# Attention in a fused two-block kernel: VectorE adds the first query tile's bias to its scores in PSUM; bias tiles laid out row by row in HBM, the second tile's bias through the identity

## The chip, the cores and the metric

The kernel runs on one core of one Trainium2 chip. The metric is the device time of one execution in microseconds; the numbers given are medians of several executions.

## The reference

Two transformer blocks run one after the other on 256 tokens of width 1024, all in float32. The first is a hybrid (state-space mixer, gated delta rule, mixture of experts). The second has four layers; each is a feed-forward half, a mixer and a second feed-forward half. The mixers alternate: layers 0 and 3 have mixer A, layer 1 a gated MLP, layer 2 mixer C. Only mixers A and C are touched.

```python
# mixer A, 16 heads of 64, chunks of 64 queries
rel  = clip(pad + i - j, -128, 128) + 128          # i: place in the query's chunk, j: place in its band of keys
s    = q @ k.T / 8 + rel_bias[:, rel]
s    = where(valid, s, -1e30); p = softmax(s); o = p @ v
# mixer C, 8 heads, each with two maps of 64
s    = q @ k.T / 8 - slope[h] * abs(qpos - kpos)
s    = where(kpos < (qpos // 64 + 1) * 64, s, -1e30); p = softmax(s)
o    = (p[:, 0] - lam * p[:, 1]) @ v
```

In both, a query sees the keys of its own 64-token chunk and of those before it. The bias depends only on the distance of query and key (and on the head), so the bias of the first 128 queries against the first 128 keys is the same tile as that of the last 128 queries against the last 128 keys.

## The kernel before, in words

Each engine has its own program, and semaphores order them. The large weights come as slabs of 128 x 2048 float32 through SyncE's DMA queue; ScalarE rounds each one to a high part (L385) and VectorE subtracts for the low part (L393), and TensorE multiplies with three products (L406 to L408). This is most of the run.

An attention stage (layers 0, 2 and 3) goes by **turns**: 8 turns of 2 heads (in layer 2: the two maps of one head). A turn g has these steps.

- `scores(g)`, TensorE, lines 2280 to 2300. For each of the 2 heads, in one PSUM bank, four float32 matmuls: the bias of the second query tile (128 queries x 256 keys) through a 128x128 constant (L2296), onto it the scores of that tile (L2297), the bias of the first query tile (128 x 128) through the same constant (L2298), onto it its scores (L2299). The constant, `turn`, is `ident` in layer 2 and `flip` (ones on the other diagonal) in layers 0 and 3. Every float32 matmul shows in the trace as two passes with a weight load each. The two heads of a turn use two banks, and two turns four banks, so `scores(g + 2)` waits for the exponentials of turn g.
- `maxes(g)`, VectorE, lines 2402 to 2408: row maxima of the second tile's scores (L2406) and of the first's (L2407), negated (L2408). The helper `done` makes VectorE wait for its own instruction before it goes on.
- `exps(g)`, ScalarE, L2367: four exponentials with row sums.
- `normalise(g)`, VectorE, lines 2410 to 2420: reciprocals (L2414; L2418 too in layer 2) and two multiplies (L2419, L2420).
- `turned(g)`, TensorE, L2310: six transposes of the probabilities; ScalarE copies them to SBUF (L2390).
- `out_of(g)`, TensorE, L2329 and L2330: the product with the values; ScalarE reads it out (L2374, or L2376 and L2377 in layer 2).

The order of the work is written out by hand for each engine. TensorE does `scores(0)`, `scores(1)`, two slabs of the projection (`mix_cols_pe`), and then for g = 0 to 7: `scores(g + 2)` while there are any, `out_of(g - 1)`, `turned(g)`. ScalarE does, for each g, the high part of a slab of the output weights (g = 0, 2, 4), the copy of the turned tiles of g, `exps(g + 2)`, the read-out of g - 1. VectorE does `normalise(g)`, the low part of that slab (g = 1, 3, 5), `maxes(g + 2)`.

The bias tiles of 2 turns (4 heads, 512 KB) lie in one of two buffers, `bias_a`. GpSimd loads them in `bias_pool` (lines 2246 to 2269) with its own DMA queue. The first two loads have no wait for a buffer; the third and the fourth wait until the turns that used the buffer have their scores (L2255). In layers 0 and 3 the table in HBM, `rel_rows`, has a row of 512 numbers for each head, and each partition reads 256 of them, one place further on than the partition before (L2260 to L2262); this puts the queries upside down, which `flip` puts right. Then GpSimd waits for the load and writes -1e30 over the keys that half of the queries don't see (L2266), and TensorE waits for that (L2285). In layer 2 the table `alibi` has whole tiles with the -1e30 in them (L2257), and TensorE waits for the load alone (L2287).

Of the kernel before, what the change touches and what calls it, by code (L numbers as in the profile page):

```python
# [19 lines left out]
ALU = mybir.AluOpType  # L20
# [3 lines left out]
P = 128  # L24
D = 1024
T = 256
# [10 lines left out]
KINDS = [i % 3 for i in range(LAYERS)]  # L37
# [205 lines left out]
def build(nc, a, out):  # L243
# [3 lines left out]
    def S(name):  # L247
        if name not in sems:
            sems[name] = ctx.enter_context(nc.semaphore(name))
        return sems[name]  # L250
# [4 lines left out]
    with ctx:  # L255
# [22 lines left out]
        rows = scratch[:, 1024:3072].rearrange("p (s n) -> p s n", s=2)  # L278
        sil = scratch[:, 3072:3584]
        h_raw = scratch[:, 3584:4096]  # L280
        mats = sb("mats", [P, len(MATS), P])
        cols = sb("cols", [P, NCOLS])
# [21 lines left out]
        psum = ctx.enter_context(nc.psum_tensor("psum", [P, 8, 512], F32))  # L304
# [3 lines left out]
        def mat(name):  # L308
            return mats[:, MATS[name], :]
# [1850 lines left out]
        SC = T + P  # L2160
# [85 lines left out]
        def bias_pool(pool, l):  # L2246
            n = ATT.index(l)

            pool.wait_ge(S("pre_rstd"), NT * (4 + 3 * l))
            for b in range(4):  # L2250
                bt = 4 * n + b
                s = bt % 2
                if bt >= 2:

                    pool.wait_ge(S("scores"), 2 * (bt - 1))  # L2255
                if KINDS[l] == 2:
                    pool.dma_start(bias_a[s], a["alibi"][:, 4 * b:4 * b + 4, :]).then_inc(S(f"bias_in{s}"), 16)  # L2257
                else:

                    tab = a["rel_rows"]  # L2260
                    base = tab.offset + ((l // 3) * 16 + 4 * b) * 512
                    pool.dma_start(bias_a[s], bass.AP(tensor=tab.tensor, offset=base, ap=[[1, P], [512, 4], [1, T]]))\  # L2262
                        .then_inc(S(f"bias_in{s}"), 16)
                    pool.wait_ge(S(f"bias_in{s}"), 16 * (bt // 2 + 1))

                    pool.memset(bias_a[s][64:P, :, 192:256], -1e30).then_inc(S("bias_ready"), 1)  # L2266
            if KINDS[l] == 0:

                pool.wait_ge(S("bias_ready"), 4 * same_before(l) + 4)
# [5 lines left out]

        def att_pe(pe, l):
            n = ATT.index(l)
            turn = mat("ident") if KINDS[l] == 2 else mat("flip")

            def scores(g):  # L2280
                gt = TURNS * n + g
                if g % 2 == 0:
                    b = 4 * n + g // 2
                    if KINDS[l] == 0:
                        pe.wait_ge(S("bias_ready"), 4 * same_before(l) + g // 2 + 1)  # L2285
                    else:
                        pe.wait_ge(S(f"bias_in{b % 2}"), 16 * (b // 2 + 1))  # L2287
                if gt >= 2:

                    pe.wait_ge(S("exp"), 4 * (gt - 1))  # L2290
                for hh in range(2):
                    h = 2 * g + hh
                    rs, c, bank = slice((h % 2) * 64, (h % 2 + 1) * 64), h // 2, 2 * (g % 2) + hh
                    bias = bias_a[(4 * n + g // 2) % 2][:, 2 * (g % 2) + hh, :]

                    pe.matmul(psum[:, bank, 0:T], turn, bias, start=True, stop=False)  # L2296
                    pe.matmul(psum[:, bank, 0:T], q_a[rs, c, P:T], k_a[rs, c, :], start=False, stop=True)  # L2297
                    pe.matmul(psum[:, bank, T:SC], turn, bias[:, P:T], start=True, stop=False)  # L2298
                    last = pe.matmul(psum[:, bank, T:SC], q_a[rs, c, 0:P], k_a[rs, c, 0:P], start=False, stop=True)  # L2299
                last.then_inc(S("scores"), 1)  # L2300

            def turned(g):
                gt = TURNS * n + g
                pe.wait_ge(S("prob"), 2 * gt + 2)

                pe.wait_ge(S("pt"), gt)
                for hh in range(2):
                    for i, at0 in enumerate((T, 0, P)):
                        e = 3 * hh + i
                        last = pe.transpose(psum[:, 4 + e // 4, (e % 4) * P:(e % 4 + 1) * P], prob_a[gt % 2][:, hh, at0:at0 + P], ident)  # L2310
                last.then_inc(S("pt_raw"), 1)

            def out_of(g):
                pe.wait_ge(S("pt"), TURNS * n + g + 1)
                if g >= 2:

                    if KINDS[l] == 0:
                        pe.wait_ge(S("act_f"), 8 * f_index(l) + g - 1)
                    else:
                        pe.wait_ge(S("att_read"), TURNS * same_before(l) + g - 1)  # L2320
                for hh in range(2):
                    p0, p1 = pt_a[:, hh * SC:hh * SC + T], pt_a[:, hh * SC + T:(hh + 1) * SC]
                    if KINDS[l] == 0:
                        h = 2 * g + hh
                        dst, vs = psum[hh * 64:(hh + 1) * 64, 6 + g % 2, 0:T], slice(h * 64, (h + 1) * 64)
                    else:
                        dst, vs = psum[:, 6 + g % 2, 0:T], slice(g * P, (g + 1) * P)
                    alone = KINDS[l] == 0
                    pe.matmul(dst, v_a[:, 0, vs], p0, start=alone or hh == 0, stop=False)  # L2329
                    last = pe.matmul(dst[:, P:T], v_a[:, 1, vs], p1, start=False, stop=alone or hh == 1)  # L2330
                last.then_inc(S("att_o"), 1)


            pe.wait_ge(S("proj_evac"), proj_base(l) + 9)
            scores(0)
            scores(1)
            mix_cols_pe(pe, l, 10, 12)
            for g in range(TURNS):
                if g == 0:
                    pe.wait_ge(S("proj_evac"), proj_base(l) + 12)  # L2340
                if g + 2 < TURNS:
                    scores(g + 2)
                if g:
                    out_of(g - 1)
                turned(g)
            out_of(TURNS - 1)
            if KINDS[l] == 2:

                pe.wait_ge(S("att_read"), TURNS * (same_before(l) + 1))
                pe.wait_ge(S("exp"), 4 * TURNS * (n + 1))  # L2350
                column_sums(pe, psum[:, 0, 0:16], o2, S("head_sums"))
                rows_of(pe, 0, sub_diag, S("head_diag"), 4 + 2 * same_before(l), S("head_rows"))
                keep_clock(pe, 7, 12)
# [46 lines left out]
        def att_dve(dve, l, done):  # L2400
            n = ATT.index(l)
            def maxes(g):
                gt = TURNS * n + g
                mx, b0 = mx_a[gt % 2], 2 * (g % 2)
                dve.wait_ge(S("scores"), gt + 1)
                dve.reduce_max(mx[:, 0:2], psum[:, b0:b0 + 2, 0:T], AX)  # L2406
                done(dve.reduce_max(mx[:, 2:4], psum[:, b0:b0 + 2, T:SC], AX))  # L2407
                dve.tensor_scalar(mx, mx, -1.0, None, ALU.mult).then_inc(S("nmax"), 1)  # L2408

            def normalise(g):  # L2410
                gt = TURNS * n + g
                inv, pr = sum_a[gt % 2], prob_a[gt % 2]
                dve.wait_ge(S("exp"), 4 * gt + 4)
                done(dve.reciprocal(inv, inv))  # L2414
                if KINDS[l] == 2:

                    odd = inv.rearrange("p (e m) -> p e m", m=2)[:, :, 1]
                    done(dve.tensor_scalar(odd, odd, nlam, None, ALU.mult))  # L2418
                dve.tensor_tensor(pr[:, :, 0:T], pr[:, :, 0:T], bc(inv[:, 0:2], T), ALU.mult).then_inc(S("prob"), 1)  # L2419
                dve.tensor_tensor(pr[:, :, T:SC], pr[:, :, T:SC], bc(inv[:, 2:4], P), ALU.mult).then_inc(S("prob"), 1)  # L2420

            maxes(0)
            maxes(1)
            for g in range(TURNS):
                normalise(g)
                if g in (1, 3, 5):
                    slab_lo(dve, f"wo{l}", g // 2)
                if g + 2 < TURNS:
                    maxes(g + 2)
            if KINDS[l] == 2:  # L2430
                dve.wait_ge(S("head_root"), same_before(l) + 3)
                done(dve.reciprocal(sub_r, sub_r))
                diagonals(dve, sub_diag, sub_r, S("head_diag"))
                dve.wait_ge(S("head_rows"), same_before(l) + 3)
                for h in range(8):
                    dve.scalar_tensor_tensor(act_f[:, h, :], act_f[:, h, :], subg, psum[:, h // 2, (h % 2) * T:(h % 2 + 1) * T], ALU.mult, ALU.mult)\
                       .then_inc(S("act_f"), 1)
# [417 lines left out]
```

## Time and profile before

| | |
|---|---|
| median of 3 executions | 2860.33 us (2856.72 to 2866.41) |
| the profiled execution | 2859.13 us, its span 2857.3 us |
| TensorE busy | 2749.0 us (96%), 14506 matmuls |
| VectorE busy | 1597.7 us (56%) |
| ScalarE busy | 1233.5 us (43%) |
| GpSimd busy | 138.2 us (5%) |
| mean granted TensorE clock | 0.982 of full |

The attention stages lie at about 1022 to 1085 us (layer 0), 2026 to 2100 us (layer 2) and 2572 to 2635 us (layer 3) of the span. Busy times of TensorE overlap with each other, since matmuls are pipelined: what a matmul costs is better read from the distance between the starts of two than from how long each is shown.

### The profile page before, as it was taken

The page shows a single profiled execution, that of the slowest core. Times are in us where ns is not written, and L with a number is a line of the kernel's source. Part 1 is how long each engine was busy: PE and PEld are TensorE (multiplying, and loading weights), DVE is VectorE, ACT ScalarE, POOL GpSimd, SP SyncE. Part 2 cuts the span into 40 slices and gives each one's busy share as a digit, 9 for nine tenths or more (in the row PEclk, how much of TensorE's full clock was granted, in tenths as well). Part 3 has the DMA queues.
Part 4 walks back from the last instruction along what each step waited for, and adds up shares of the span by engine and source line. Part 5 has one row for each costly group of instructions (what it writes and reads, how often), then busy time and mean ns, then how long its engine had stood idle before and what let it go on. Part 6 is the DMA issues. An engine that isn't in the chain of part 4 may idle for free. (4 is left out here: it accounts for less than half of the span.)

```text
span 2857.3 us, 35303 instructions
## 1 busy us (share of the span) xinstructions
PE 2749.0 (96%) x14506; PEld 2305.6 (81%) x14506; DVE 1597.7 (56%) x1821; ACT 1233.5 (43%) x1588; POOL 138.2 (5%) x227
## 2 busy tenths in 40 slices
PE   7988889999999999999998999999999999999998
PEld 6977877888788877888887888888878888896887
DVE  5884477776644535455554556455454554544544
ACT  3202256665534445344344435344453444445443
POOL 3000000000000100001000000000000010000000
PEclk9998989999999999999999999999999999999999
DMA  7532067887555435646544655554436555452652
GB/s 251 161 104 89 30 224 268 294 306 276 194 197 186 141 125 178 205 154 229 177 162 140 214 178 191 196 192 140 136 119 201 191 181 193 162 170 89 221 177 89
DMA packets 349485, 509.35 MB, mean 178 GB/s; under 512 B 14880, under 2 KB 295488, under 8 KB 349328
## 3 DMA queue, kind: packets, MB, share of 16 engines
q1 hardware_dynamic: 342960, 484.17, 50.4%
q0 software_dynamic: 5792, 20.78, 2.1%
q8 instruction: 112, 1.84, 0.3%
q10 hardware_dynamic: 576, 2.20, 0.2%
q14 instruction: 45, 0.37, 0.0%
HBM read 506.04 MB, written 1.05 MB: 177 GB/s over the span
## 5 line engine op out<-in xcount | busy, mean ns | idle before, releaser
L393 DVE TENSOR_TENSOR raw_r<-raw,whi 128x2048 fp32r<-128x2048 f32 x185 | 421.8, 2290 | 168.0 <-ACT whi L385 167.2
L833 ACT ACTIVATE h_hi<-psum 128x256 fp32r<-128x256 f32 x216 | 82.8, 383 | 758.1 <-PE psum L772 684.1
L385 ACT ACTIVATE whi<-raw 128x2048 fp32r<-128x2048 f32 x185 | 351.1, 1909 | 13.0 <-DMA raw<-in_w_up 7.4
L888 DVE TENSOR_TENSOR h_lo<-psum,h_hi 128x256 fp32r<-128x256 f32 x216 | 91.5, 423 | 439.0 <-ACT h_hi L833 439.0
L407 PE MATMUL psum<-place_lo,act_hi 128*128 128x512 f32 (+1 forms) x840 | 318.6, 379 | 0.0
L406 PE MATMUL psum<-whi,act_hi 128*128 128x512 f32 (+1 forms) x872 | 308.7, 354 | 5.4 <-DVE act_lo L639 4.3
L408 PE MATMUL psum<-whi,act_lo 128*128 128x512 f32 (+1 forms) x872 | 302.7, 347 | 0.0
L393 DVE TENSOR_TENSOR place_lo<-arena,place_hi 128x2048 fp32r<-128x2048 f32 x107 | 244.2, 2290 | 90.7 <-ACT place_hi L385 90.7
L407 PE MATMUL psum<-raw_r,act_hi 128*128 128x512 f32 (+1 forms) x808 | 284.2, 352 | 0.0
L406 PE MATMUL psum<-place_hi,act_hi 128*128 128x512 f32 (+1 forms) x592 | 234.1, 395 | 0.0
L408 PE MATMUL psum<-place_hi,act_lo 128*128 128x512 f32 (+1 forms) x592 | 228.6, 386 | 0.0
L406 PE MATMUL psum<-wlo,act_hi 128*128 128x512 f32 (+1 forms) x520 | 192.5, 370 | 13.4 <-DVE act_lo L639 9.5
L385 ACT ACTIVATE place_hi<-arena 128x2048 fp32r<-128x2048 f32 x107 | 202.8, 1907 | 0.5 <-DMA arena<-in_ff_w_in 0.5
L408 PE MATMUL psum<-wlo,act_lo 128*128 128x512 f32 (+1 forms) x520 | 187.5, 361 | 0.0
L406 PEld LDWEIGHTS psum<-whi,act_hi 128*128 128x128 f32 x872 | 166.4, 191 | 24.8 <-issue 4.8
L408 PEld LDWEIGHTS psum<-whi,act_lo 128*128 128x128 f32 x872 | 166.3, 191 | 21.0
L407 PEld LDWEIGHTS psum<-place_lo,act_hi 128*128 128x128 f32 x840 | 158.0, 188 | 29.1
L393 DVE TENSOR_TENSOR wlo<-wlo_f,wlo 128x2048 fp32r<-128x2048 f32 x61 | 139.7, 2290 | 74.4 <-ACT wlo L385 73.7
L407 PEld LDWEIGHTS psum<-raw_r,act_hi 128*128 128x128 f32 x808 | 154.5, 191 | 18.5
L826 ACT ACTIVATE scratch<-psum 128x256 f32<-128x256 f32 x216 | 82.1, 380 | 183.8 <-PE psum L408 183.7
L406 PE MATMUL psum<-act_hi,whi 128*128 128x256 f32 x496 | 142.1, 286 | 8.1 <-DVE act_lo L601 5.9
L407 PE MATMUL psum<-raw_r,h_hi 128*128 128x512 f32 x372 | 145.4, 391 | 0.0
(537 smaller groups left out, 5820.6 us busy)
## 6 DMA issues: line engine op xcount, KB each, us to landing
arena<-in_ff_w_in SPq DMA_DIRECT2D x182, 512.0 KB, 5.0
raw<-in_ff_w_in SPq DMA_DIRECT2D x126, 512.0 KB, 4.8
arena<-in_ff_w_out SPq DMA_DIRECT2D x88, 512.0 KB, 4.5
raw<-in_ff_w_out SPq DMA_DIRECT2D x68, 512.0 KB, 4.4
wlo_f<-in_ff_w_in SPq DMA_DIRECT2D x44, 512.0 KB, 4.9
raw<-in_w_ada SPq DMA_DIRECT2D x20, 1024.0 KB, 5.2
raw<-in_w_gate SPq DMA_DIRECT2D x35, 512.0 KB, 4.4
raw<-in_w_up SPq DMA_DIRECT2D x35, 512.0 KB, 5.7
```

Of the source, the lines that this page charges most:

```text
L385: act.activation(hi, loaded, ACT.Copy).then_inc(S("slab_hi"), 1)
L393: dve.tensor_tensor(lo, loaded, hi.bitcast(F32), ALU.subtract).then_inc(S("slab_lo"), 1)
L406: pe.matmul(out_ap, lhs[0], rhs[0], start=first, stop=False)
L407: pe.matmul(out_ap, lhs[0], rhs[1], start=False, stop=False)
L408: return pe.matmul(out_ap, lhs[1], rhs[0], start=False, stop=last)
L826: act.activation(pair_of(sil, g), gate_up(g)[:, 0:256], ACT.Silu).then_inc(S("pass_sil"), 1)
L833: act.activation(pair_of(turned_h[0], g), gate_up(g)[:, 0:256], ACT.Copy).then_inc(S("pass_turned_hi"), 1)
L888: dve.tensor_tensor(pair_of(turned_h[1], g), gate_up(g)[:, 0:256], pair_of(turned_h[0], g).bitcast(F32), ALU.subtract)\
```

## The change

For each head, TensorE no longer puts the first query tile's bias into PSUM (the old L2298); its scores (L2299) now open their region. VectorE adds the bias to the scores of both heads of the turn in place, in PSUM, before it takes the maxima. The second tile's bias goes through `ident` in all layers. The table of layers 0 and 3 now holds whole tiles of 128 x 256, queries the right way up, and the mask falls on partitions 0 to 63. Since VectorE now reads the bias buffer too, the third and fourth loads also wait for `nmax`, which is set at the end of `maxes`.

```diff
                 if bt >= 2:
                     pool.wait_ge(S("scores"), 2 * (bt - 1))
+                    pool.wait_ge(S("nmax"), 2 * (bt - 1))
...
-                    tab = a["rel_rows"]
-                    base = tab.offset + ((l // 3) * 16 + 4 * b) * 512
-                    pool.dma_start(bias_a[s], bass.AP(tensor=tab.tensor, offset=base, ap=[[1, P], [512, 4], [1, T]]))\
-                        .then_inc(S(f"bias_in{s}"), 16)
+                    head = (l // 3) * 16 + 4 * b
+                    pool.dma_start(bias_a[s], a["rel_tiles"][:, head:head + 4, :]).then_inc(S(f"bias_in{s}"), 16)
                     pool.wait_ge(S(f"bias_in{s}"), 16 * (bt // 2 + 1))
-                    pool.memset(bias_a[s][64:P, :, 192:256], -1e30).then_inc(S("bias_ready"), 1)
+                    pool.memset(bias_a[s][0:64, :, 192:256], -1e30).then_inc(S("bias_ready"), 1)
...
-            turn = mat("ident") if KINDS[l] == 2 else mat("flip")
...
-                    pe.matmul(psum[:, bank, 0:T], turn, bias, start=True, stop=False)
+                    pe.matmul(psum[:, bank, 0:T], ident, bias, start=True, stop=False)
                     pe.matmul(psum[:, bank, 0:T], q_a[rs, c, P:T], k_a[rs, c, :], start=False, stop=True)
-                    pe.matmul(psum[:, bank, T:SC], turn, bias[:, P:T], start=True, stop=False)
-                    last = pe.matmul(psum[:, bank, T:SC], q_a[rs, c, 0:P], k_a[rs, c, 0:P], start=False, stop=True)
+                    last = pe.matmul(psum[:, bank, T:SC], q_a[rs, c, 0:P], k_a[rs, c, 0:P], start=True, stop=True)
...
                 mx, b0 = mx_a[gt % 2], 2 * (g % 2)
+                bias = bias_a[(4 * n + g // 2) % 2][:, 2 * (g % 2):2 * (g % 2) + 2, P:T]
                 dve.wait_ge(S("scores"), gt + 1)
+                done(dve.tensor_tensor(psum[:, b0:b0 + 2, T:SC], psum[:, b0:b0 + 2, T:SC], bias, ALU.add))
                 dve.reduce_max(mx[:, 0:2], psum[:, b0:b0 + 2, 0:T], AX)
...
-    rel = v["a_rel_bias_2"][:, :, np.clip(255 - np.arange(512), -128, 128) + 128]
+    rel = v["a_rel_bias_2"][:, :, np.clip(P + np.arange(P)[:, None] - np.arange(T)[None, :], -128, 128) + 128]
...
-        "b_b_s": v["b_b_s_2"].reshape(1, -1), "cols": cols, "rows": rows, "gains": gains, "rel_rows": rel.reshape(-1, 512), "mats": mats,
+        "b_b_s": v["b_b_s_2"].reshape(1, -1), "cols": cols, "rows": rows, "gains": gains, "rel_tiles": rel.reshape(-1, P, T).transpose(1, 0, 2), "mats": mats,
```

## Rows read from the trace of the kernel before

**Rows 1.** The page's busy time of each engine over the run.
```profile
PE 2749.0 (96%) x14506; PEld 2305.6 (81%) x14506; DVE 1597.7 (56%) x1821; ACT 1233.5 (43%) x1588; POOL 138.2 (5%) x227
```

**Rows 2.** Busy time by stretch: from:to, us, engines (instructions), granted clock, DMA share, GB/s.
```profile
1022.00:1043.00 21.00, 20.71 (x136) 16.89 (x134) 3.59 (x9) 6.06 (x20) 1.06 (x2) 1.00 0.37 126
1043.00:1085.00 42.00, 37.26 (x208) 23.21 (x208) 22.25 (x44) 25.28 (x71) 1.60 (x3) 1.00 0.15 51
...
2047.00:2100.00 53.00, 47.37 (x242) 33.70 (x243) 25.77 (x52) 27.81 (x78) 1.04 (x2) 0.97 0.12 40
```

**Rows 3.** What TensorE waited for, 970 us to the end: total us, times, longest.
```profile
PE psum L2329 <- ACT arena L2390: 8.1, 9, 0.9
```

**Rows 4.** Timeline of TensorE, layer 0, turn 5's scores to turn 6's: start, us.
```profile
1059.47 0.60 PE L2296 MATMUL psum<-arena,mats 128*128 128x256 f32 x2
1060.00 0.70 PE L2297 MATMUL psum<-arena 64*128 64x256 f32 x2
1060.63 0.49 PE L2298 MATMUL psum<-arena,mats 128*128 128x128 f32 x2
1061.05 0.48 PE L2299 MATMUL psum<-arena 64*128 64x128 f32 x2
1061.46 0.70 PE L2296 MATMUL psum<-arena,mats 128*128 128x256 f32 x2
1062.09 0.70 PE L2297 MATMUL psum<-arena 64*128 64x256 f32 x2
...
1063.55 0.66 PE L2329 MATMUL psum<-arena 128*64 128x256 f32 x4
...
1065.07 0.60 PE L2296 MATMUL psum<-arena,mats 128*128 128x256 f32 x2
```

**Rows 5.** The removed matmul's line over the whole run: ns min/median/max.
```profile
L2298 PE MATMUL psum<-arena,mats x96: 275/326/377, 1023.8 to 2624.0; 128*128 128x128 f32 x96
```

**Rows 6.** Groups of VectorE over the run that read PSUM: busy us, mean ns.
```profile
L888 DVE TENSOR_TENSOR h_lo<-psum,h_hi 128x256 fp32r<-128x256 f32 x216 | 91.5, 423 | 439.0 <-ACT h_hi L833 439.0
L723 DVE TENSOR_TENSOR arena<-psum,scratch 128x512 f32<-128x512 f32 x48 | 32.5, 688 | 36.7 <-ACT scratch L703 36.7
```

**Rows 7.** Timeline of VectorE, layer 0: maxima of turns 3 to 5, normalising and a slab.
```profile
1052.47 0.69 DVE L2406 TENSOR_REDUCE small<-psum 128x2 f32<-128x512 f32 x1 [0.22 <-PE psum L2299]
...
1058.06 0.69 DVE L2406 TENSOR_REDUCE small<-psum 128x2 f32<-128x512 f32 x1 [3.23 <-PE psum L2299]
...
1059.20 0.17 DVE L2414 RECIPROCAL small<-small 128x4 f32<-128x4 f32 x1
...
1060.35 2.28 DVE L393 TENSOR_TENSOR raw_r<-raw,whi 128x2048 fp32r<-128x2048 f32 x1
1063.66 0.69 DVE L2406 TENSOR_REDUCE small<-psum 128x2 f32<-128x512 f32 x1 [1.02 <-PE psum L2299]
```

**Rows 8.** Timeline of ScalarE, layer 0: copy of turn 2, exponentials of turn 4, copy of turn 4.
```profile
1059.67 0.81 ACT L2390 ACTIVATE arena<-psum 128x768 f32<-128x768 f32 x1 [1.10 <-PE psum L2310]
1060.38 0.47 ACT L2367 ACTIVATE arena<-psum,small 128x256 f32<-128x256 f32 x1
...
1061.97 0.40 ACT L2374 ACTIVATE act_f<-psum 128x256 f32<-128x256 f32 x1
...
1070.86 0.81 ACT L2390 ACTIVATE arena<-psum 128x768 f32<-128x768 f32 x1 [1.10 <-PE psum L2310]
```

**Rows 9.** Timeline of TensorE at the end of layer 0's turns.
```profile
1074.74 0.66 PE L2329 MATMUL psum<-arena 128*64 128x256 f32 x4
...
1078.13 0.87 PE L2310 MATMUL psum<-mats,arena 128*128 128x128 f32 x6
```

**Rows 10.** Timeline of GpSimd, layer 0, the fourth bias load.
```profile
1052.73 0.75 POOL L2262 DMA_DIRECT2D arena<-in_rel_rows  x1 [17.00 <-PE psum L2299]
1056.64 0.31 POOL L2266 MEMSET arena<- 64x256 f32 x1 [3.16 <-DMA arena<-in_rel_rows]
```

**Rows 11.** The loads of L2257 (whole tiles, layer 2): us from issue to landing.
```profile
DMA to landing us min/median/max: 3.7/4.8/6.6
```

## The prediction

> **What bounds the kernel now.** The page says that TensorE is shown busy for 2749 us of the span [rows 1], so I look first at what lies on its path in the attention stages. The list of its waits has one entry there that matters: 8.1 us in 9 places, 3 in each stage, for the copy of turned tiles when no scores are left to do [rows 3]. Between scores, products and transposes it waits for nothing. So I read a turn off its timeline, by starts, because the shown durations overlap. From the scores of turn 5 at 1059.47 to those of turn 6 at 1065.07 it is 5.60 us [rows 4], of which the scores take 4.08, the product and the transposes 1.52. VectorE and ScalarE are idle for part of every turn: VectorE for 3.23 us of a turn without a slab and 1.02 us of one with a slab [rows 7], ScalarE for 1.10 us of a turn with a slab [rows 8]. The stage is bound by TensorE's instruction stream, turn after turn, except at its end.
>
> **TensorE.** The change takes L2298 out: 96 passes, two for each of 48 heads [rows 5]. Its distance to the next instruction is 1060.63 to 1061.05, 0.42 us a head, and that of L2299 is 0.41, both of 128 columns; those of L2297 (1060.00 to 1060.63) and of L2296 behind L2299 are 0.63, with 256 columns [rows 4]. So each pass costs 0.21 us with 128 columns and 0.315 with 256, whatever stood before it: half of the difference, 0.105, is what 128 columns cost, and about another 0.105 is cost that doesn't depend on the columns, the weight load that isn't covered. I take the whole 0.42, since L2299's weights must still be loaded behind L2297 as they now are behind L2298. 48 x 0.417 = **20.0 us**. The bounds: if the part that isn't columns stays behind as a wait, only 2 x 0.105 = 0.21 a head goes, 10.1 us in all; if the gap behind L2297 goes as well, it is 0.63 a head, 30 us. `flip` to `ident` costs nothing: the same shape of matmul runs with either (in layer 2 it is `ident` now).
>
> A page prices this step lower. The Trainium skill, "TensorE: Matmul & The Clock Gate", section "Back-to-back issue gap", puts a sustained stream of weight load and matmul at about 81 ns for 128 columns. As an estimate from that page 96 passes would be 7.8 us. The trace disagrees, 0.21 us a pass [rows 4]; these are float32 passes, and the measurement decides.
>
> The first two turns' scores come before two slabs of the projection, not in the loop; TensorE is busy for 20.71 of 21.00 us there, at clock 1.00 [rows 2], so they save as much. That makes 8 turns in each of 3 stages, 0.83 us each.
>
> **VectorE.** 24 adds of 128 x 256, in PSUM, with the bias from SBUF. No row writes float32 back to the PSUM that it reads. The nearest row has the same size and one operand in PSUM, 423 ns (L888); an add of 128 x 512 takes 688 ns (L723) and is my upper end, no cost beyond start-up (0.16, the two rows carried to no columns) the lower [rows 6]. I take 0.42, and 0.46 with the wait of `done`: 24 x 0.46 = 11 us of VectorE. Is it covered? Between its starts of `maxes` VectorE works 5.59 - 3.23 = 2.36 us in a turn without a slab and 5.60 - 1.02 = 4.58 in one with [rows 7]; with the add 2.82 and 5.04, 3.93 on the mean, against a new turn of 5.60 - 0.83 = 4.77. A slab turn is thus 0.27 us over; the next maxima start that late and the following turn makes it up. The maxima of turn 4 are done 1.14 us after they start, at 1059.20 [rows 7], and the exponentials start only at 1060.38, behind the copy [rows 8]: 1.18 us to spare, against 0.46 + 0.27 = 0.73. So ScalarE doesn't notice. The tightest is turn 3, whose maxima had 0.22 us to spare behind the first slab [rows 7]: 0.46 + 0.83 - 0.22 = 1.07 late, plus the add, 1.53 against 1.18. Its exponentials come 0.35 us late. Who waits? `scores(5)`. In turn 4 the exponentials end at 1061.97 [rows 8] and the scores that need their bank start at 1065.07 [rows 4], 3.10 apart, 2.27 after the change, 1.9 with the lateness. Nothing on TensorE. In layer 2 a turn is longer (its product isn't packed) and has more room.
>
> At the end, when `scores(7)` is done (1074.74), TensorE reaches `turned(6)` 3.39 us later (1078.13) [rows 9]. VectorE must by then have the maxima of 7 and the normalising of 6: 0.11 for the signal + 0.27 + 0.46 + 1.14 + 1.15 = 3.13 [rows 4, 7]. That is 0.26 us inside. With an add of 0.72 (the 688 ns row) and the lateness of 0.53 it would be 0.26 outside: 0.8 us over three stages, my upper end. I put it at nothing.
>
> **ScalarE.** No instruction changes. With a slab it has 1.10 us to spare [rows 8], 0.27 after the change.
>
> **GpSimd and its queue.** As many loads of 512 KB, now with one run of 4 KB for each partition in place of four of 1 KB; the first two are early. The third has turns to spare. The fourth has to be looked at, for it now waits for `nmax` of turn 3. Today it is issued at 1052.73 and masked at 1056.64 + 0.31 [rows 10], and `scores(6)` needs it at 1065.07 [rows 4]: 8.1 us to spare. Two blocks of scores shorter, 1.67, and an issue 1.07 + 0.46 + 1.14 + 0.11 = 2.8 later leave 3.7. The load and its wait take 3.9 now; whole tiles in layer 2 took 3.7 to 6.6 [rows 11], so at worst 2.7 more, still inside. Behind it on GpSimd is the load of the gains, which nothing uses before the output weights are done. Cost: none.
>
> **The sum.** 2859.13 - 20.0 = 2839.1 for an execution like the profiled one, whose time is 1.2 below the median of the three; so **2840 us**. What follows a stage is bound by TensorE as well and moves forward with it.
>
> **The rivals.**
> 1. *Only the columns are saved.* The weight load that L2298 hid or carried is exposed behind L2297. For it: 0.105 of every pass isn't columns. Against it: that part is equal behind passes of 128 and 256 columns. 2860.3 - 10.1 = 2850.
> 2. *The add is on the path.* If every turn's scores, add, maxima, exponentials and next scores formed the bound, a turn would gain 0.83 - 0.46 = 0.37, 8.9 us in all: 2851. Against it: 1.18 us to spare ahead of the exponentials, 3.10 behind them. It takes an add of well over 1 us.
> 3. *Slower: the fourth bias load becomes the wait.* Place: `scores(6)` in each stage. It costs from a landing of 3.9 + 3.7 = 7.6 us on, one for one, three times. It eats the whole gain at 7.6 + 6.7 = 14.3, and gives over 8.6 us more than now at 17: 2869. The worst landing seen of this form is 6.6, with few other transfers in these stages (DMA share 0.12 to 0.15) [rows 2].
> 4. *Slower: the clock.* The granted clock was 1.00 in the turns of layer 0, and 0.97 in layer 2's stretch, which takes in its idle end [rows 2]. At half clock a new turn's 8 passes of 256 and 4 of 128 columns alone would add 8 x 0.21 + 4 x 0.105 = 2.1 us, 24 times 50 us: 2890. The same skill page, Part 4, says that transposes don't count as busy for the clock; they lie within the 1.52 us of a turn that stay, so their share grows a little, and the 1.00 of today's turns gives no reason to fear it.
>
> **Chances and range.** Forecast 0.86, rival 1 0.05, rival 2 0.05, rivals 3 and 4 together 0.03, a gain near the 30 us bound 0.01. The three executions shown are 10 us apart, so the median of a few may be 3 to 4 off whatever the mechanism; with the small terms at the end of a stage the range is 2834 to 2849, just short of rivals 1 and 2. About 0.3% (8.6 us) is what a measurement of this kernel can tell from no change. Rivals 1 and 2 lie just beyond that, so part of their chance counts as the same: faster 0.94, same 0.03, slower 0.03.
>
> **What would show it.** Right: turns of 4.77 us in layer 0 (5.60 now), 0.63 from L2297 to L2299, no wait of TensorE ahead of the scores, adds of about 0.42 us, the wait for copies still near 8 us in 9 places. Wrong: L2297 to L2299 over 0.8 (rival 1); TensorE waiting for ScalarE ahead of scores (2) or for GpSimd's mask ahead of turn 6 (3); a granted clock below 1 (4). I would also be wrong if the stretches between attention stages got longer, since I take them to move unchanged.

## The result, and the profile after

The changed kernel takes 2832.91 us (median of 6 executions, 2828.9 to 2836.21); the kernel before, run beside it, 2862.03 (6 executions). The ratio is 0.9896, 95% interval 0.9884 to 0.9908: 29 us less, where I had forecast 20 and a range that ended at 2834. The direction was right, and so was what bounds the stages; the price of what TensorE no longer does was not, and the gain was half as large again.

The page of the changed kernel, engines' busy time (for [rows 1]):

```profile
span 2827.1 us, 35143 instructions
...
PE 2718.9 (96%) x14410; PEld 2295.7 (81%) x14410; DVE 1606.8 (57%) x1845; ACT 1232.8 (44%) x1588; POOL 136.8 (5%) x227
```

96 matmul passes fewer, 24 VectorE instructions more. All of the gain is in the three attention stages. From the first bias matmul of a stage to its last product (L2330, now L2326), by their starts on TensorE's timeline:

| kernel | layer 0 | layer 2 | layer 3 | sum | rest of the span |
|---|---|---|---|---|---|
| before | 60.41 | 64.93 | 60.41 | 185.7 | 2671.6 |
| changed | 50.79 | 55.14 | 50.78 | 156.7 | 2670.4 |

The rest of the span differs from one profile to the next (2668 to 2682 us over the 14 kernels of this study), and most of the difference lies ahead of the first stage, which begins between 1022.7 and 1031.9 us. The stages come out alike to 0.01 us where nothing in them changed (e4_layout_only below), so I read their lengths first and the medians as their check.

Busy time by stretch for the three stages of the changed kernel, columns as in [rows 2]:

```profile
1023.00:1073.00 50.00, 46.50 (x298) 35.38 (x298) 28.36 (x59) 29.63 (x86) 2.20 (x5) 1.00 0.30 95
2016.00:2071.00 55.00, 51.61 (x305) 41.74 (x304) 30.20 (x67) 30.49 (x92) 1.57 (x3) 1.00 0.26 87
2552.00:2603.00 51.00, 47.51 (x306) 35.97 (x305) 28.36 (x59) 29.85 (x86) 2.19 (x5) 1.00 0.29 93
```

The granted clock, the last number but two, is 1.00 in all three. What TensorE waited for from 965 us on (for [rows 3]) is the same list as before, the copies at the end of the stages with the same 8.1 us:

```profile
PE psum L2325 <- ACT arena L2386: 8.1, 9, 0.9
...
PE psum L2293 <- ACT arena L2229: 2.1, 3, 0.7
```

TensorE's timeline of one turn (for [rows 4]; L2293 to L2295 are the bias of the second tile, its scores and the first tile's scores):

```profile
1053.33 0.60 PE L2293 MATMUL psum<-arena,mats 128*128 128x256 f32 x2
1053.86 0.70 PE L2294 MATMUL psum<-arena 64*128 64x256 f32 x2
1054.40 0.38 PE L2295 MATMUL psum<-arena 64*128 64x128 f32 x2
1054.71 0.70 PE L2293 MATMUL psum<-arena,mats 128*128 128x256 f32 x2
1055.34 0.70 PE L2294 MATMUL psum<-arena 64*128 64x256 f32 x2
1055.87 0.38 PE L2295 MATMUL psum<-arena 64*128 64x128 f32 x2
1056.18 0.66 PE L2325 MATMUL psum<-arena 128*64 128x256 f32 x4
...
1057.70 0.38 PE L2293 MATMUL psum<-arena,mats 128*128 128x256 f32 x1
```

A turn is 4.37 us, not the 4.77 I forecast. The removed L2298 took its 0.42 a head with it, and two distances beside it shrank: from the second tile's scores to the next matmul 0.54 (0.63 before), from the first tile's scores to what follows 0.31 (0.41 before). 0.42 + 0.09 + 0.10 = 0.61 a head, 48 heads, 29.3 us; the stages lost 29.0 (e3_no_add below accounts for the difference).

VectorE's timeline, from the slab of turn 3 to the maxima of turn 6 (for [rows 7]; L2403 is the new add):

```profile
1054.67 2.28 DVE L393 TENSOR_TENSOR raw_r<-raw,whi 128x2048 fp32r<-128x2048 f32 x1
1056.87 0.42 DVE L2403 TENSOR_TENSOR psum<-psum,arena 128x256 f32<-128x256 f32 x1
1057.33 0.69 DVE L2404 TENSOR_REDUCE small<-psum 128x2 f32<-128x512 f32 x1
...
1060.66 0.43 DVE L2403 TENSOR_TENSOR psum<-psum,arena 128x256 f32<-128x256 f32 x1 [0.96 <-PE psum L2295]
```

The add takes 0.42 to 0.43 us and 0.46 until the next instruction, as assumed. Behind a slab it starts with no idle time before it, 0.69 us after the scores of turn 5 are done (1056.18), and one turn later VectorE waits for TensorE again.

GpSimd's fourth bias load in layer 0 (for [rows 10]):

```profile
1051.18 0.53 POOL L2262 DMA_DIRECT2D arena<-in_rel_tiles  x1 [16.18 <-DVE small L2406]
1055.12 0.30 POOL L2265 MEMSET arena<- 64x256 f32 x1 [3.41 <-DMA arena<-in_rel_tiles]
```

It now waits for VectorE's negated maxima; issue to mask is 3.9 us, as before, and the tile is ready 2.3 us before the scores of turn 6 (1057.70), where I had worked out 3.7.

### The profile page after: what moved, and what is told of

Its sections match the earlier page's. It is cut to its first block and busy times, and to the rows that moved or that the text cites. A ratio compares the mean times of both kernels' runs of the same rounds, so it can differ in the third digit from the quotient of the medians.

```text
span 2827.1 us, 35143 instructions
## 1 busy us (share of the span) xinstructions
PE 2718.9 (96%) x14410; PEld 2295.7 (81%) x14410; DVE 1606.8 (57%) x1845; ACT 1232.8 (44%) x1588; POOL 136.8 (5%) x227
```

## The experiments

The open question was the extra 0.2 us a head. **Theory S**: a matmul that uses another set of array rows than the one before it (128 rows for a bias, 64 for scores) costs about 0.2 us beyond its columns, 0.1 ahead of its first pass and 0.1 between its two; L2298 stood between two matmuls of 64 rows and made two such changes. **Theory W**: the cost belongs to L2298 as an instruction. **Theory G**: the rest came from the new layout and its loads. Beside that I tested the three places where I had said that something is covered: VectorE's time, the fourth bias load, the clock.

| run | layer 0, 2, 3 | median us | ratio to before, 95% interval |
|---|---|---|---|
| e1_pairs | 49.05, 53.57, 49.05 | 2831.58 | 0.9884 (0.9868 to 0.9901) |
| e2_half_rows | 54.18, 58.71, 54.18 | 2845.29 | 0.9934 (0.9917 to 0.9951) |
| e3_no_add | 50.61, 55.13, 50.61 | 2828.33 | 0.9890 (0.9869 to 0.9910) |
| e4_layout_only | 60.41, 64.93, 60.41 | 2859.86 | 0.9997 (0.9987 to 1.0007) |
| e5_grouped | 46.56, 49.26, 49.08 | 2819.77 | 0.9866 (0.9848 to 0.9884) |
| e6_interleaved | 46.52, 49.23, 48.66 | 2822.41 | 0.9875 (0.9850 to 0.9900) |
| e7_three_adds | 57.65, 61.12, 57.66 | 2853.33 | 0.9976 (0.9964 to 0.9987) |
| e8_inter_no_add | 44.67, 47.53, 44.67 | 2810.11 | 0.9833 (0.9815 to 0.9852) |
| e9_late_load | 61.28, 63.77, 60.48 | 2861.58 | 0.9997 (0.9988 to 1.0007) |
| e10_late_slab | 45.56, 48.90, 45.56 | 2816.14 | 0.9842 (0.9822 to 0.9861) |
| e11_two_adds | 54.70, 55.14, 53.85 | 2840.24 | 0.9915 (0.9895 to 0.9935) |
| e12_clock_kept | 45.57, 48.90, 45.57 | 2816.76 | 0.9840 (0.9817 to 0.9863) |

### What a change of rows costs

**e2_half_rows**, the kernel before with one matmul narrowed:

```diff
-                    pe.matmul(psum[:, bank, T:SC], turn, bias[:, P:T], start=True, stop=False)
+                    pe.matmul(psum[:, bank, T:SC], turn[rs, :], bias[rs, P:T], start=True, stop=False)
```

> The kernel before, with L2298 over the 64 rows that the head's L2297 and L2299 use instead of all 128; this leaves out the bias of half of the first tile's queries, at the same number of matmuls and columns. Theory S: 2 changes of rows a head instead of 4, L2297 to L2298 0.53 us instead of 0.63, L2298 to L2299 0.22 instead of 0.42, 0.4 a head less and so 2862 - 19.5 = about 2842. Theory W: 2862, distances as before.

Measured: TensorE's timeline of e2_half_rows, one head,

```profile
1059.94 0.60 PE L2296 MATMUL psum<-arena,mats 128*128 128x256 f32 x2
1060.47 0.70 PE L2297 MATMUL psum<-arena 64*128 64x256 f32 x2
1061.00 0.38 PE L2298 MATMUL psum<-arena,mats 64*128 64x128 f32 x2
1061.22 0.38 PE L2299 MATMUL psum<-arena 64*128 64x128 f32 x2
1061.54 0.70 PE L2296 MATMUL psum<-arena,mats 128*128 128x256 f32 x2
```

The same matmuls with the same columns: 0.53 from L2297, 0.22 from L2298, 0.32 from L2299, against 0.63, 0.42 and 0.41 in [rows 4]. The stages lose 18.7 us together, 0.39 a head, as theory S says, and the median 16.4. L2298's weights still come from another tensor, so it is the rows that count. Theory W falls.

Where the time goes can be seen in the weight loads of the changed kernel (PEld's timeline):

```profile
1049.49 0.29 PEld L2294 LDWEIGHTS psum<-arena 64*128 64x128 f32 x2 [0.33 <-issue]
1049.81 0.40 PEld L2295 LDWEIGHTS psum<-arena 64*128 64x128 f32 x2
1050.34 0.30 PEld L2293 LDWEIGHTS psum<-arena,mats 128*128 128x128 f32 x2
```

L2294's load starts with L2294's first pass (1049.49 on both timelines): nothing was loaded ahead. L2295's starts at 1049.81, while L2294's second pass runs, and L2295 itself starts 0.22 us later (1050.03). The Trainium skill, "TensorE: Matmul & The Clock Gate", Part 3, section "What overlaps and what doesn't", says that a weight load overlaps a running matmul only where the row groups differ. This trace doesn't bear out the "only": with the same 64 rows on both sides the load is under the matmul. From 128 rows to 64 or back the groups differ but share rows, and the load isn't covered. Groups that share no rows do overlap as the page says: in e1_pairs below, the second head's first load starts less than 0.01 us behind the first head's first pass.

**e4_layout_only**, the changed kernel with the add taken out and L2298 put back:

```diff
+                    pe.matmul(psum[:, bank, T:SC], ident, bias[:, P:T], start=True, stop=False)
-                    last = pe.matmul(psum[:, bank, T:SC], q_a[rs, c, 0:P], k_a[rs, c, 0:P], start=True, stop=True)
+                    last = pe.matmul(psum[:, bank, T:SC], q_a[rs, c, 0:P], k_a[rs, c, 0:P], start=False, stop=True)
...
-                done(dve.tensor_tensor(psum[:, b0:b0 + 2, T:SC], psum[:, b0:b0 + 2, T:SC], bias, ALU.add))
```

> The change's data layout alone: whole tiles in HBM, ident, the mask on the other half, GpSimd's second wait; TensorE puts the first tile's bias in by itself as before, no add. Theories S and W: 2862, no change. Theory G (some of the unexpected 10 us comes from the loads or their waits): between 2852 and 2860.

Measured: every stage as long as before to 0.01 us, ratio 0.9997. Theory G falls: whole tiles, `ident`, the other mask and GpSimd's second wait are worth nothing either way.

**e1_pairs**, the kernel before, its matmuls in another order:

```diff
-                    pe.matmul(psum[:, bank, 0:T], turn, bias, start=True, stop=False)
-                    pe.matmul(psum[:, bank, 0:T], q_a[rs, c, P:T], k_a[rs, c, :], start=False, stop=True)
-                    pe.matmul(psum[:, bank, T:SC], turn, bias[:, P:T], start=True, stop=False)
-                    last = pe.matmul(psum[:, bank, T:SC], q_a[rs, c, 0:P], k_a[rs, c, 0:P], start=False, stop=True)
+                for rs, c, bank, bias in heads:
+                    pe.matmul(psum[:, bank, 0:T], turn, bias, start=True, stop=False)
+                for rs, c, bank, bias in heads:
+                    pe.matmul(psum[:, bank, 0:T], q_a[rs, c, P:T], k_a[rs, c, :], start=False, stop=True)
+                for rs, c, bank, bias in heads:
+                    pe.matmul(psum[:, bank, T:SC], turn, bias[:, P:T], start=True, stop=False)
+                for rs, c, bank, bias in heads:
+                    last = pe.matmul(psum[:, bank, T:SC], q_a[rs, c, 0:P], k_a[rs, c, 0:P], start=False, stop=True)
```

> The kernel before, its four matmuls of each head kept, but issued for both heads of a turn side by side: bias, bias, scores, scores, bias, bias, scores, scores. Theory S (a matmul that uses another set of array rows, 128 or 64, than the one before it costs about 0.2 us beyond its columns, because its weights are not loaded under the one before): 4 changes of rows a turn instead of 8, so 4 x 0.2 x 24 = 19 us less than before, about 2843, and more if the two 64-row matmuls, on different halves of the array, run at the same time. Theory W (the 0.62 a head was what L2298 costs as an instruction, whatever stands beside it): no change, 2862.

Measured: 2831.58, as fast as the changed kernel (whose ratio, 0.9896, lies in this one's interval), with no VectorE work and no new layout; its stages are 5.0 us shorter yet, which the medians can't tell. TensorE's timeline of e1_pairs, one turn's scores:

```profile
1059.03 1.03 PE L2296 MATMUL psum<-arena,mats 128*128 128x256 f32 x4
1059.98 0.70 PE L2298 MATMUL psum<-arena 64*128 64x256 f32 x4
1060.62 0.71 PE L2300 MATMUL psum<-arena,mats 128*128 128x128 f32 x4
1061.26 0.49 PE L2302 MATMUL psum<-arena 64*128 64x128 f32 x4
1061.68 0.66 PE L2332 MATMUL psum<-arena 128*64 128x256 f32 x4
```

2.65 us for the scores (4.08 before). The four bias passes take 0.95, of which 0.1 is the change of rows at their end. The four passes of 64 rows take 0.64 and 0.42, what two took in [rows 4]: the two heads lie on different halves of the array and run side by side. Of the 1.43 us, 0.8 is four changes of rows fewer and 0.6 the overlap.

**e5_grouped** and **e6_interleaved**, the changed kernel with both bias matmuls of a turn first; e5 then goes head after head, e6 alternates:

```diff
+                    pe.matmul(psum[:, heads[hh][2], 0:T], ident, bias_a[(4 * n + g // 2) % 2][:, 2 * (g % 2) + hh, :], start=True, stop=False)
+                for rs, c, bank in heads:
+                    pe.matmul(psum[:, bank, 0:T], q_a[rs, c, P:T], k_a[rs, c, :], start=False, stop=True)
+                    last = pe.matmul(psum[:, bank, T:SC], q_a[rs, c, 0:P], k_a[rs, c, 0:P], start=True, stop=True)
```

(This is e5; e6 has a second `for` line between the last two.)

> The changed kernel with a turn's two bias matmuls first, then the four 64-row ones, head after head. Theory S: 2 changes of rows a turn instead of 4, 0.4 us less, a turn of 3.97 us instead of 4.37, just over VectorE's mean of 3.93 for two turns with one slab; 9.7 us less than the changed kernel, about 2823. If a change to the other half of the array costs as much as one from 128 to 64 rows: 4.8 us less, 2828. Theory W: 2833, no change.

> As e5_grouped, but the 64-row matmuls of the two heads alternate, so that each pair lies on both halves of the array. In e1_pairs such pairs started 0.007 us apart, so TensorE's scores should take 1.8 us a turn (2.86 in the changed kernel) and its turn 3.3. If TensorE still bound the turn: 25 us less, 2808. I expect VectorE to bind at its mean of 3.93 (add, maxima, normalising, half a slab), with waits of TensorE ahead of the scores or the transposes: 10 to 15 us less than the changed kernel, 2818 to 2823.

Measured: 2819.77 and 2822.41, stages alike (46.56 and 46.52 in layer 0). e5 beat its expectation because its heads overlap too. TensorE's timeline of e5_grouped:

```profile
1058.76 1.03 PE L2292 MATMUL psum<-arena,mats 128*128 128x256 f32 x4
1059.72 0.71 PE L2294 MATMUL psum<-arena 64*128 64x256 f32 x4
1060.26 0.40 PE L2295 MATMUL psum<-arena 64*128 64x128 f32 x4
1061.40 0.66 PE L2325 MATMUL psum<-arena 128*64 128x256 f32 x4 [0.75 <-ACT arena L2386]
```

The program has L2294 and L2295 of the first head, then both of the second, and the trace shows all four passes of L2294 and then all four of L2295: the second head's start before the first head's L2295. The scores are 1.8 to 1.9 us now, but in this turn TensorE then waits 0.75 us for a copy.

### Where VectorE binds

**e3_no_add** takes the add out of the changed kernel, **e8_inter_no_add** out of e6_interleaved, **e11_two_adds** and **e7_three_adds** repeat it:

```diff
-                done(dve.tensor_tensor(psum[:, b0:b0 + 2, T:SC], psum[:, b0:b0 + 2, T:SC], bias, ALU.add))
```

> The changed kernel without VectorE's add (the first tile's bias is left out). If the add is covered, as I argued: 2833, within 1 us of the changed kernel. If part of it is on the path: up to 11 us less, 2822. Nothing here depends on theories S and W.

Measured: the stages 0.36 us shorter in all than the changed kernel's. The add is all but covered: 11 us of VectorE cost 0.4 us of time. The median is 4.6 us below the changed kernel's, but the intervals overlap (0.9869 to 0.9910 and 0.9884 to 0.9908), and the stages say that this isn't the add. What is left lies at one place, the transposes of turn 6 in layers 0 and 3, 0.18 us each. TensorE's timeline there, first the changed kernel,

```profile
1067.99 0.40 PE L2326 MATMUL psum<-arena 128*64 128x128 f32 x4
1068.49 0.88 PE L2306 MATMUL psum<-mats,arena 128*128 128x128 f32 x6
```

then e3_no_add:

```profile
1069.56 0.40 PE L2326 MATMUL psum<-arena 128*64 128x128 f32 x4
1069.89 0.87 PE L2306 MATMUL psum<-mats,arena 128*128 128x128 f32 x6
```

The transposes need VectorE's normalising of turn 6, which comes behind the third slab and the maxima of turn 7.

> e6_interleaved without the add (the first tile's bias is left out). If VectorE binds in e6_interleaved, taking 0.46 us a turn from it gives back 5 to 9 us against e6_interleaved, until ScalarE (mean 3.55 a turn) or the chain of one turn binds: 2811 to 2816. If TensorE binds there: the same time as e6_interleaved.

Measured: 2810.11, the stages 7.5 us shorter than e6_interleaved's, in the range. VectorE is on TensorE's path there: in layer 0 the waits for its normalising fall from 2.1 to 0.7 us, the stage from 46.52 to 44.67. Layer 3 gains 4.0 us, more than the others (1.9 and 1.7), because e6 lost the clock at its end and e8 didn't.

> The changed kernel with the add twice (the first tile's bias counts double). VectorE's mean of two turns with one slab becomes 4.39 us, TensorE's is 4.37. If VectorE's total decides: no wait inside the turns, and only at the end the transposes of turn 6 wait about 1 us (0.11 + 1.13 + 0.92 + 1.14 + 1.15 = 4.45 us after the last scores, against 3.39): 3 us in all, 2836. If each add is on the path: 11 us more, 2844.

> The changed kernel with the add three times (the first tile's bias counts threefold). VectorE's mean of two turns with one slab rises from 3.93 by 0.92 to 4.85 us, over TensorE's 4.37. If VectorE's total is what decides: 0.48 us more in each of some 5 turns of a stage, and the lateness at the end, 2 to 4 us a stage, 2839 to 2845. If each add is on the path anyway (rival 2 of the prediction): 0.92 in all 24 turns, 22 us, 2855. If VectorE has more room than I count: 2833.

Measured: 2840.24 and 2853.33, the stages 7.0 and 19.7 us longer than the changed kernel's. For e7 I had 6 to 12, for e11 3, or 11 with each add on the path, so both came out above what VectorE's total gives; e7's result alone looks like rival 2 (22 us). It isn't that. e11, with half the extra adds, has layer 2 unchanged at 55.14, and its turns in layer 0 stay at TensorE's pace until the end. TensorE's timeline of e11_two_adds at the end of layer 0:

```profile
1074.01 0.87 PE L2306 MATMUL psum<-mats,arena 128*128 128x128 f32 x6
1075.78 0.66 PE L2325 MATMUL psum<-arena 128*64 128x256 f32 x4 [0.90 <-ACT arena L2386]
...
1078.06 1.42 PE L2306 MATMUL psum<-mats,arena 128*128 128x128 f32 x6 [1.40 <-DVE arena L2419]
1080.37 1.13 PE L2325 MATMUL psum<-arena 128*64 128x256 f32 x4 [0.90 <-ACT arena L2386]
```

One wait of 1.40 us for VectorE, where I had worked out 1.06, and there the same six transposes are 1.42 us long instead of 0.87: the granted clock has gone to 0.50, the lower of its two levels (1.2 GHz). Stretches of e11_two_adds:

```profile
1060.00:1070.00 10.00, 9.93 (x63) 6.87 (x64) 9.69 (x21) 8.56 (x30) 1.36 (x3) 1.00 0.34 105
1070.00:1080.00 10.00, 7.17 (x45) 4.84 (x43) 8.96 (x19) 7.94 (x23) 0.00 (x0) 0.91 0.00 1
1080.00:1085.00 5.00, 3.73 (x18) 2.45 (x20) 0.00 (x0) 1.68 (x4) 0.00 (x0) 0.50 0.00 0
```

So the stage grows by 3.9 us for a wait of 1.4. In e7 the same: the stretch at the end of layer 0's stage in e7_three_adds,

```profile
1080.00:1090.00 10.00, 6.37 (x30) 4.13 (x31) 2.41 (x5) 5.03 (x14) 0.00 (x0) 0.50 0.01 2
```

TensorE waited 4.2 us for VectorE in that stage, in three places, and the stage is 6.9 us longer.

### The fourth bias load, and the clock behind a wait

**e9_late_load**:

```diff
-                    pool.wait_ge(S("nmax"), 2 * (bt - 1))
+                    pool.wait_ge(S("nmax"), 2 * (bt - 1) + (2 if b == 3 else 0))
```

> The changed kernel, with GpSimd's fourth bias load waiting for the maxima of turn 5 instead of turn 3. In the changed kernel the tile is masked at 1055.42 and the scores of turn 6 start at 1057.70: 2.3 us to spare in layer 0. The maxima of turn 5 come 7.9 us after those of turn 3, so TensorE should wait 5.7 us for GpSimd in layers 0 and 3 and about 4.6 us for the DMA in layer 2 (rival 3 of the prediction, one for one beyond the spare time): 16 us more than the changed kernel, about 2849, and more if the clock falls after the wait.

Measured: 2861.58; the stages are 28.8 us longer in all than the changed kernel's, where I had 16. The wait itself is as worked out. TensorE's timeline of e9_late_load:

```profile
1072.71 1.22 PE L2293 MATMUL psum<-arena,mats 128*128 128x256 f32 x2 [5.70 <-POOL arena L2265]
1073.86 1.22 PE L2294 MATMUL psum<-arena 64*128 64x256 f32 x2
1074.87 0.63 PE L2295 MATMUL psum<-arena 64*128 64x128 f32 x2
```

5.70 us, and then the bias matmul's distance to the next is 1.15 in place of 0.53 to 0.63. The granted clock of the 10 us slices shows why:

```profile
1060.00:1070.00 10.00, 7.01 (x45) 4.86 (x44) 8.47 (x17) 9.13 (x31) 0.53 (x1) 0.96 0.06 7
1070.00:1080.00 10.00, 7.29 (x22) 4.47 (x23) 1.66 (x5) 1.54 (x1) 0.83 (x2) 0.50 0.29 98
1080.00:1090.00 10.00, 8.20 (x48) 5.69 (x48) 7.05 (x14) 6.24 (x22) 0.00 (x0) 0.86 0.00 1
```

A late load is not paid one for one but at 1.8 times its wait in layers 0 and 3 (5.70 and 5.46 us, the stages 10.5 and 9.7 longer) and at 2.0 times in layer 2 (4.41 us, 8.6 longer). The whole gain of the change is lost by a load that comes two turns late.

### A faster version

**e10_late_slab**, e5_grouped with VectorE's third slab moved behind its last normalising, and **e12_clock_kept**, e10 with idle matmuls in the waits at the end:

```diff
-                if g in (1, 3, 5):
-                    slab_lo(dve, f"wo{l}", g // 2)
+                if g in (1, 3, 7):
+                    slab_lo(dve, f"wo{l}", {1: 0, 3: 1, 7: 2}[g])
...
                 turned(g)
+                if g >= 6:
+                    keep_clock(pe, 0, 4)
             out_of(TURNS - 1)
+            if KINDS[l] == 0:
+                keep_clock(pe, 0, 6)
```

(The part above the dots is e10's, the part below is what e12 adds.)

> e5_grouped with the low part of the third output-weight slab taken by VectorE after the last normalising instead of before the maxima of turn 7. VectorE binds in e5_grouped, and after its last normalising it is idle for 4 us. If VectorE's work ahead of the last turns is what sets the end: up to 2.2 us a stage less, 2813 to 2817 against about 2820. If ScalarE's copies set it: no change.

> e10_late_slab with idle matmuls in the waits at the end of a stage: four 128-column ones (0.85 us) after the transposes of turns 6 and 7 and six before the output weights in layers 0 and 3. In e5_grouped and e6_interleaved the granted clock fell to half at the end of layer 3's stage (0.70 and 0.62 in two slices of 10 us) and that stage took 2.5 us longer than layer 0's. If the waits let it fall: clock 1.00 there, all stages alike, and up to 2.5 us less than e10_late_slab where it shows the fall. If it doesn't fall in e10_late_slab: the same time or up to 1 us more.

Measured: 2816.14 for e10, ratio 0.9842, with e12 the fastest of the kernels that compute all of the reference; its interval and the changed kernel's don't meet. The stages lose 1.0, 0.4 and 3.5 us against e5_grouped; most of the last is the clock, which e5 had lost at the end of layer 3 and e10 keeps. Stretch of layer 3's stage, in e5_grouped

```profile
2542.00:2591.00 49.00, 41.94 (x304) 33.15 (x304) 28.34 (x59) 29.85 (x86) 2.19 (x5) 0.93 0.30 97
```

and in e10_late_slab

```profile
2542.00:2588.00 46.00, 39.67 (x306) 31.56 (x304) 28.43 (x59) 29.77 (x87) 2.20 (x5) 1.00 0.32 103
```

e12 gives the same stages to 0.01 us. One of its four executions took 10.7 ms, for which these runs give no reason; the median of the other three is 2814.83, and the two kernels can't be told apart by time. With the clock at 1.00 in e10's stages already, the idle matmuls have nothing to keep there. Behind layer 3 they have: the 10 us after the stage, first in e10_late_slab, then in e12_clock_kept,

```profile
2588.00:2598.00 10.00, 8.37 (x57) 8.40 (x58) 4.83 (x6) 6.29 (x10) 0.00 (x0) 0.83 0.47 147
2585.00:2595.00 10.00, 9.71 (x83) 9.37 (x80) 5.48 (x6) 6.91 (x11) 0.00 (x0) 1.00 0.50 156
```

That is the one place where a run shows filled waits and a kept clock against idle waits and a lost one; behind layer 0 the clock stayed at 1.00 in both, and behind layer 2, where e12 fills only the waits of the last turns, both lost it (0.71 and 0.68 over 10 us). Why e5's layer 0 kept its clock and layer 3, with the same work and the same waits, didn't isn't settled by these runs.

## Why the prediction was wrong, point by point

- **What bounds the kernel**: right. The turns ran at TensorE's pace before and after, the list of waits is the same, and everything outside the stages stayed within 1.2 us.
- **TensorE's 20.0 us**: this term was mis-sized; it measures 29.3 by the distances, 29.0 by the stages. The step that failed is "each pass costs 0.21 us with 128 columns and 0.315 with 256, whatever stood before it", and from it "L2299's weights must still be loaded behind L2297 as they now are behind L2298". The 0.105 beyond the columns isn't a cost of a pass. It is the price of a change between 128 and 64 rows (e2: 0.39 us a head for two changes fewer, with all matmuls kept), and before the change every score matmul had such a change on both sides. The row that told otherwise was in [rows 4]: the first L2296 of the turn, behind transposes of 128 rows too, takes 0.53 where the second takes 0.63. I had named the outcome as a bound, "if the gap behind L2297 goes as well, it is 0.63 a head, 30 us", and gave it 1 in 100; nothing in the trace spoke against it at those odds, because no row showed two matmuls of 64 rows in a row.
- **The Trainium skill's 7.8 us**: further off than the trace's 20.
- **VectorE**: right on the add, 0.42 us, 0.46 with its wait, and on its being covered in the turns. The end of a stage I had put at nothing, 0.26 us inside; it costs 0.18 in layers 0 and 3, 0.4 us in all (e3). The turn is 0.4 us shorter than I took it to be, so the slab ahead of turn 7's maxima ends later against the scores, and the maxima start 0.69 us behind them, not 0.38. VectorE is nearer to the bound than I said, 3.93 against 4.37: e11 finds the edge with one more add.
- **Rival 1, only the columns saved**: refuted by the distances. **Rival 2, the add on the path**: refuted by e3. **Rival 3, the fourth load**: its place is right, with 2.3 us to spare in the changed kernel and not 3.7; its price isn't one for one (e9). (Even one for one, a landing of 17 us would give 8.2 us more than now, not "over 8.6".) **Rival 4, the clock**: did not come in the changed kernel, 1.00 in all three stages; it is what makes the late waits in e7, e9 and e11 dear.
- **`flip` to `ident`, layout, GpSimd's wait at nothing**: right (e4).

## What to carry to other kernels

Where matmuls of different row counts alternate, price the columns of each and then the changes of rows, not a fixed cost for each matmul: here a change cost 0.2 us, about what the columns of a 128-column float32 matmul cost, and reordering alone (e1) was worth as much as the whole change. Put matmuls that use opposite halves of the array, and different banks, next to each other. And when an engine behind TensorE has little room left, price a wait of TensorE above its length, since the clock can fall with it.

## What the runs showed of the hardware that I had not expected

- A change between 128 and 64 rows costs about 0.2 us beside the columns, half ahead of the first pass of the matmul behind it and half between its two passes: 0.42 for L2298 with a change before and after it, 0.22 with neither; 0.63 for L2297 with both, 0.53 with only the one before ([rows 4] and e2_half_rows). A change of columns alone shows a gap too: in the changed kernel's layer 0 the transposes (128*128) start 0.32 us behind the first pass of L2326 (128*64), in its layer 2, where L2326 is 128*128 as well, 0.22.
- Matmuls of two heads on the two 64-row halves of the array, into different banks, take the time of one (e1: 0.64 us for four passes of 256 columns), and the second head's matmul starts ahead of a matmul that stands before it in the program (e5). The same holds for the two 64-column halves: L2329 shows four passes in a row in [rows 4], though the program has the first head's L2330 after two of them.
- In e11 the granted clock went to 0.50 at a wait of 1.4 us close behind one of 0.9 and stayed there for the rest of the stage, while three waits of 0.9 us a stage leave it at 1.00 in the changed kernel. The length of one wait doesn't decide it: a wait of 1.22 us in e5's layer 0 left it at 1.00, and e5's layer 3 lost it at its end, behind waits of 0.9.
